# Paged attention of the sample group: the value products of a unit move from two units behind the scores to one

## The reference, cut to what matters

```
def page_step(carry, pages):
    rows = cache[layer, pages]
    logits = jnp.einsum('bqhc,bkc->bqhk', qc, rows).astype(jnp.float32) * MLA_SCALE
    return update(carry, logits, rows[..., :MLA_KV_LORA]), None
...
def update(carry, logits, vals):
    m, l, acc = carry
    m_new = jnp.maximum(m, jnp.max(logits, axis=-1))
    corr = jnp.exp(m - m_new)
    p = jnp.exp(logits - m_new[..., None])
    l = l * corr + jnp.sum(p, axis=-1)
    acc = acc * corr[..., None] + jnp.einsum('bqhk,bkc->bqhc', p, vals.astype(jnp.float32))
    return (m_new, l, acc)
```

## Time and profile before

| | us |
|---|---|
| median of 3 runs | 2490.68 |
| lowest and highest of them | 2480.44 and 2490.76 |
| the profiled execution, its own time | 2497.16 |
| its span, first to last instruction | 2495.4 |
| first gather of the stage issued, at | 826.45 |
| last copy of values of the stage ends, at | 1124.68 |

### The profile page before, as it was taken

One profiled execution on the slowest core, in us unless ns is written; L12 is line 12 of the kernel. 1 busy time (PEld: TensorE's weight loads), 2 busy tenths in 40 slices (PEclk: granted clock), 3 DMA queues, 4 the chain that ended last, 5 costly groups with the idle time before them and its releaser, 6 DMA issues. The chain is left out here.

```text
span 2495.4 us, 40033 instructions
## 1 busy us (share of the span) xinstructions
PE 2200.5 (88%) x17388; PEld 1927.9 (77%) x17388; DVE 1064.6 (43%) x1402; ACT 522.3 (21%) x954; POOL 73.0 (3%) x132
## 2 busy tenths in 40 slices
PE   6999968838999588885899988877999999999997
PEld 6999936724677455554799888657999999999997
DVE  4212145564666576771222233556422332422433
ACT  3101014411343222230111122224111111111110
POOL 0000000000400011100000000000000000000000
PEclk8999968769999888996899999977999999999998
DMA  5113050030992567765111111301111111111111
GB/s 186 46 46 123 21 167 30 33 107 20 303 331 75 228 248 281 284 240 160 62 46 46 53 40 55 118 1 34 43 51 43 51 49 45 43 51 43 44 50 77
DMA packets 179011, 247.96 MB, mean 99 GB/s; under 512 B 23219, under 2 KB 164507, under 8 KB 173516
## 3 DMA queue, kind: packets, MB, share of 16 engines
q1 hardware_dynamic: 166992, 162.04, 20.9%
q0 software_dynamic: 5904, 83.95, 8.9%
q10 hardware_dynamic: 5996, 0.25, 0.2%
HBM read 220.35 MB, written 69.87 MB: 116 GB/s over the span
## 5 line engine op out<-in xcount | busy, mean ns | idle before, releaser
L1188 PE MATMUL ps<-mla_rt,q_now 32*32 32x256 f32 x4608 | 153.4, 407 | 51.8 <-DVE mla_rt L1282 43.9
L1282 DVE STREAM_TRANSPOSE mla_rt<-mla_rows 128x1536 f32<-128x1536 f32 x96 | 164.6, 1752 | 44.1 <-DMA mla_rows<-in_cache_mla,page_rows 43.6
L2336 PE MATMUL ps<-xn_hi,mlp_w_hi 128*128 128x344 f32 x768 | 164.2, 322 | 7.3 <-DVE mlp_w_lo L2150 5.3
L1188 PEld LDWEIGHTS ps<-mla_rt,q_now 32*32 32x32 f32 x4608 | 96.8, 110 | 90.6 <-issue 69.2
L2336 PE MATMUL ps<-mlp_xn_lo,mlp_w_hi 128*128 128x344 f32 x768 | 163.7, 321 | 0.0
L2336 PE MATMUL ps<-u_lo,mlp_w_hi 128*128 128x344 f32 x768 | 163.0, 320 | 0.0
L2336 PE MATMUL ps<-xn_hi,mlp_w_lo 128*128 128x344 f32 x768 | 162.9, 320 | 0.0
L2336 PE MATMUL ps<-u_hi,mlp_w_hi 128*128 128x344 f32 x768 | 162.9, 320 | 0.0
L2336 PE MATMUL ps<-u_hi,mlp_w_lo 128*128 128x344 f32 x768 | 162.1, 319 | 0.0
L2336 PEld LDWEIGHTS ps<-xn_hi,mlp_w_hi 128*128 128x128 f32 x768 | 129.8, 190 | 8.9 <-DVE mlp_w_lo L2150 6.4
L2336 PEld LDWEIGHTS ps<-u_lo,mlp_w_hi 128*128 128x128 f32 x768 | 130.0, 189 | 0.0
(11 more groups left out here) (376 smaller groups left out, 3693.9 us busy)
## 6 DMA issues: line engine op xcount, KB each, us to landing
out_s_dsa_w<-in_cache_dsa_w SPq DMA_DIRECT2D x8, 4094.0 KB, 80.5
oaT<-in_w_up SPq DMA_DIRECT2D x32, 512.0 KB, 4.1
oaT<-in_w_down SPq DMA_DIRECT2D x32, 512.0 KB, 3.8
obT<-in_w_in SPq DMA_DIRECT2D x23, 512.0 KB, 3.7
gate_w<-in_w_in SPq DMA_DIRECT2D x16, 512.0 KB, 4.1
out_s_dsa_w<-in_cache_dsa_w SPq DMA_DIRECT2D x8, 1022.0 KB, 16.3
s_kv_tile<-in_cache_dsa_w SPq DMA_DIRECT2D x12, 512.0 KB, 5.6
x_scr<-qkvT SPq DMA_DIRECT2D x1, 4128.0 KB, 15.4
```

Source lines behind the costliest of these rows:

```text
L1188: last = nc.tensor.matmul(ps[32 * (JG * s + g):32 * (JG * s + g) + 32, i, 0:JN * SQ], q_now[SQ * i:SQ * i + SQ, s, c, :], rt[SQ * i:SQ * i ...
L1282: nc.vector.transpose(rt[:, k * n:(k + 1) * n], rows[:, v, :, k * n * SQ:(k + 1) * n * SQ].rearrange("p n (c f) -> p c n f", c=n)).then_in ...
L2336: last = nc.tensor.matmul(out[:, t, 0:TC], w, x[:, k, t * TC:(t + 1) * TC], start=first, stop=stop)
```

## The change

TensorE's list for unit u becomes: thirds 0 and 1 of the scores of u, turned probabilities of u - 1, third 2 of the scores of u, values of u - 1. VectorE turns thirds 0 and 1 of u + 1 ahead of the maximum of u, and third 2 behind it. ScalarE copies the values of u - 1, behind the exponential of u, where it had copied those of u - 2 ahead of the copy of the probabilities. Buffers, semaphores, the number of instructions and GpSimd's and SyncE's lists are as they were; a gather still waits for the values of the unit four before.

```diff
@@ TensorE
                 def unit(u, v):
-                    score(u, v % 2, 0, 1)
-                    if not isinstance(u, int) or u >= 2:
-                        value(u - 2, v % 2, (v - 2) % UPB)
-                    if not isinstance(u, int) or u >= 1:
+                    first = isinstance(u, int) and u == 0
+                    score(u, v % 2, 0, CG - 1)
+                    if not first:
                         turn_probs(u - 1, (v - 1) % 2)
-                    score(u, v % 2, 1, CG)
+                    score(u, v % 2, CG - 1, CG)
+                    if not first:
+                        value(u - 1, (v - 1) % 2, (v - 1) % UPB)
...
-                value(NU - 2, (NU - 2) % 2, (NU - 2) % UPB)
                 turn_probs(NU - 1, (NU - 1) % 2)
                 value(NU - 1, (NU - 1) % 2, (NU - 1) % UPB)
@@ ScalarE
                 for u in range(NU):
-                    if u >= 2:
-                        copy_values(u - 2)
                     if u:
                         copy_probs(u - 1)
                     exp(u)
+                    if u:
+                        copy_values(u - 1)
                     if u + 2 < NU:
                         query(u + 2)
-                copy_values(NU - 2)
                 copy_probs(NU - 1)
                 copy_values(NU - 1)
@@ VectorE
                 for u in range(NU):
                     if u + 1 < NU:
-                        turn(u + 1, 0)
+                        for k in range(CG - 1):
+                            turn(u + 1, k)
                     row_max(u)
                     if u + 1 < NU:
-                        for k in range(1, CG):
-                            turn(u + 1, k)
+                        turn(u + 1, CG - 1)
```

## The result

The changed kernel takes 2456.7 us, the median of 4 runs (2453.2 to 2462.6); before it was 2490.7 (2480.4 to 2495.4). The ratio is 0.987, with a 95% interval of 0.984 to 0.990: 34 us or 1.3% faster. The forecast was 2441.3, a gain of 49.4, with a range from 2425 to 2465. The direction was right, and so was the ring that the forecast follows; the gain was some 15 us too large.

A forecast was written before the change was run, and what follows sets the result against it. The prediction took page attention to be bound by a gather-to-values cycle, 8.8 us a unit, falling to 6.9. Gains of 3.3 (start), 44.2 (middle) and 1.9 (end) made 49.4 us: 2441.3 us forecast, range 2425 to 2465.

The forecast's parts named there:

- the ring: Page attention's cycle from values' end through gather, turns and scores to values' end: 17.6 us for two units before.
- (a): GpSimd's gather leaves earlier: that of u + 3 goes at the start of u + 1, one unit further ahead, less part.
- (b): Page attention's new cycle, from values of u - 1 to values of u + 2: 20.66 us, three units, 6.9 each.
- R3: Rival, page attention: gathers in flight slow each other; landing 12.7 us, 7.7 a unit, 2464 us in all; chance 0.08.
- (c): ScalarE's copy of the probabilities, between turned probabilities and values: hidden by 0.6 us; uncovered, 19 us would be added.
- (d): VectorE's third turn behind the maximum: ready 3.5 us later while TensorE has 5.2 us of work, hidden by 1.7.
- (e): Next bounds in page attention, per unit: VectorE 6.6 us, TensorE 6.5, DMA engines 6.5 or 5.8; all below 6.9.
- (f): TensorE's three issue gaps early in the stage, 3.74, 4.04 and 3.87 us: taken for code loading, all kept.
- R1: Rival, TensorE: four to six more code-loading gaps of 3.9 us, giving 2457 to 2465 us; chance 0.13.
- The sum: Page attention's forecast gain: start 3.3, middle 44.2, end 1.9, in all 49.4 us, from the median to 2441.3.
- middle term: Fifth gather to the one at 1090.74, 26 units: 231.5 us before, 187.3 after with two gaps, 44.2 gained.
- The stage has nothing that varies so much: Reason for taking the profiled execution's page-attention gain, 49.4 us, from the median too, though that execution was 6.5 above it.

## Why the prediction was right, and where it was not

- **What bounds the kernel:** right. The ring over the gather, two units long; a delay in it showed once for two units, and without gathers the orders differ by 5 us.
- **(a), (b), the new ring of three units:** right in its parts, with one of them too short. I took 10.18 us from gather to first turn. Where VectorE waits for a gather from unit 12 on, the first trace of the changed kernel has 10.3 to 11.6, 10.8 in the mean; the median landing rose from 10.0 to 10.7 us (10.5 in the second trace). (10.5 + 10.8) / 3 = 7.10 against 7.11 measured and 6.9 predicted. This is R3 in a mild form. Over 26 units it is 5.5 us.
- **(c) and (d), hidden copy and third turn:** right. ScalarE's copy held the values once, for 0.7 us, at the stage's end; TensorE waited for turns only at its start.
- **(e), the next bounds:** TensorE's own time is 6.70 and not 6.5 us. It pays about 0.1 at each change from one kind of matmul to another: the third of the scores between turned probabilities and values takes 1.46, not 1.33.
- **(f), the issue gaps:** about right in sum, 9.3 and 10.4 where I kept 11.7, though seven shorter ones. That the old kernel has three of 3.9 was already of one trace. R1 in its strong form did not come: none in later passes.
- **The sum** was mis-sized in its middle term, 44.2. The changed kernel's middle took 194.5 and 196.6 us in its two traces, not 187.3: 5.5 of the 8.3 by the landing, the rest in the early units, where some steps between gathers are still 10 to 12 us long. And the old kernel's middle was 231.5, 221.0 and 223.5 in three traces; the one used was 6.2 above their mean. Together 14.5, and the middle gained 29.8. Start and end gained 3.9 and 2.4 against 3.3 and 1.9, as differences of means; in the old kernel alone the start took 28.6 to 32.8 and the end 33.7 to 38.4.
- **"The stage has nothing that varies so much"** was the step that failed. It is just the stage that varied, by 12 us between traces of one program. The third trace shows its two paces, with long pauses and a slow clock or with neither. In the two traces of the changed kernel the stage has one pace, 254.9 and 255.8, and its runs lie closer together, from 2450.6 to 2465.2 in ten, where the old kernel's in the same batches lie from 2474.6 to 2503.5.
- What was not seen at all is how the gain divides. From 8.57 a unit, the mean of the three old traces, 0.74 goes when the pauses are merely spread and the clock stays up, in a ring still of two units (7.83), and the other 0.72 by the third unit in the ring (7.11). The 7.83 is of one trace, the fastest run of its ten; the first part of the old kernel's third trace, 7.88, agrees with it. I had named the clock as a part of what a late gather costs, but had put no price on it. The forecast held without one, because it took the old stage as measured, slow stretches and all, and the new ring from rows at the full clock.

## What to carry to other kernels

Follow a buffer around: from the instruction that frees it over the refill to the one that frees it again, and count how many units one round serves. Time a unit is the round divided by that count, so that a unit more in the ring is worth more than a shorter step in it; a known delay put into the ring shows the count in the steps between refills. Where TensorE must wait, several short waits may cost less than a long one: look at the granted clock behind each. And take the base of a sum from more than one trace of the stage.

## What the runs showed of the hardware

- Pauses of some 2.0 to 3.5 us in every second unit went with a mean clock of 0.90 to 0.93 in the old kernel, though not each was followed by the slow clock; pauses up to about 1 us in each unit left it at 1.00 (VectorE's order alone, and the changed kernel), and so did 0.5 and 1.8 us in turn (the old kernel's third trace, 914 to 966 us).
- The median landing time of a 2.36 MB gather was 9.7 to 10.2 us in the traces with a DMA share of 0.69 to 0.87 from 930 to 1080 (9.7 at 0.87, VectorE's order alone), and 10.5 to 10.7 in those with 0.89 to 0.94.
- "Issue" gaps of TensorE, 5 to 12 us a stage and nearly all in newly entered code, vanish (under 0.6) when no gathers are in flight.
- The time from the start of the program to this stage spread over 13.6 us between executions, and went with the mean clock from 400 to 560 us: 0.66 to 0.70 in the six early traces, 0.59 to 0.63 in the seven late ones. What decides that clock was not looked into.
